# Adding the squared chunks in pairs on GpSimd ahead of the column sums of five norms

## The chip, the cores and the metric

The kernel runs on one core of a Trainium2 chip. The metric is device time in microseconds (us) of that core. The core has five engines that run side by side and meet at semaphores: TensorE (PE in the profile; its weight loads are PEld), VectorE (DVE), ScalarE (ACT), GpSimd (POOL) and SyncE (SP), which here only issues transfers.

## The reference, cut to what matters

A two-layer block works on x of 256 tokens by 1024 features, all in fp32. Each layer applies three sublayers, and each sublayer begins with the same norm, so there are six norms (numbered 0 to 5 here, 3 per layer).

```
def rms_norm(x, gain):
    y = xf * lax.rsqrt(jnp.mean(xf * xf, axis=-1, keepdims=True) + EPS)
    return y * gain
...
for l in range(2):
    h = modulate(rms_norm(x, norm_g[l, 0]), sh1, sc1); x = x + 0.5 * g1 * swiglu(h, ...)
    h = modulate(rms_norm(x, norm_g[l, 1]), sh2, sc2); x = x + g2 * token_mix(h, ...)
    h = modulate(rms_norm(x, norm_g[l, 2]), sh3, sc3); x = x + 0.5 * g3 * swiglu(h, ...)
```

The mean over the 1024 features is what the change touches: the sum of the squares of eight chunks of 128 features, for each token.

## The kernel before

**Layout.** x is kept transposed in `xT`, 128 partitions by 8 chunks by 256 tokens: a partition is one feature of a chunk. A "bank" b of a norm is the pair of chunks 2b and 2b+1, because a sublayer's output for those two chunks fills PSUM bank b. Weights come in slabs of 128x2048, numbered in the order of use; each is split into a high part (`w_hi`, by ScalarE, L1005) and a low part (`w_lo = raw - w_hi`, by VectorE, L1484), and TensorE makes three products for each tile of weights.

**The way into a norm (norms 1 to 5).** When bank b of the sublayer's output is done, VectorE adds it to `xT` (L1561, two instructions for a bank). ScalarE then squares the bank into `hf` (L1029, one instruction of 128x512) and makes `xm_hi` from it (L1031, one for each chunk), and VectorE makes `xm_lo` (L1507, one for each chunk). TensorE multiplies `hf` by a 128x128 matrix of ones (L637, function `sums`), which adds over the partitions, and accumulates the eight chunks in PSUM bank 0. While the norm's factor is not known yet, TensorE already works on the first slabs with the unnormalized `xm` (function `lead`, L650). ScalarE loads a table (L1018), splits a slab (L1005) and forms the factor `rstd` (L1012, L1014), VectorE splits a slab (L1484) and then normalizes chunk by chunk (L1541, L1546).

**Where the sums stand in TensorE's order.** Norms 1, 3 and 4 follow a feed-forward: its last output block calls `sums(norm, 0)` after its tile 5 and `sums(norm, 1)` after its tile 7, and `lead` takes banks 2 and 3 after its third chunk. Norms 2 and 5 follow the token mixing: the third of the four last slabs (K_OUT+2) is followed by `sums(norm, 0, 1)`, the fourth (K_OUT+3) by `sums(norm, 2)`, and `lead` takes bank 3.

**Order.** Every engine's order is written out by hand, and every engine executes its own queue in order, so a waiting instruction holds all behind it. GpSimd builds constants at the start, masks `bias` once (L470, L471), and in each layer clears and masks a small tile (L477, L483: `affine_select` of 64x128, twice for each of four heads). Norm 0 has its own code and is not changed.

Of the kernel before, what the change touches and what calls it, by code (L numbers as in the profile page):

```python
# [11 lines left out]
ALU = mybir.AluOpType  # L12
# [3 lines left out]
DEPTH = 2  # L16
# [89 lines left out]
def build(nc, x, c, w_ada, b_ada, norm_g, w_ff_in, w_ff_out, w_in, qk_norm_g, attn_sinks, rel_bias,  # L106
# [3 lines left out]
    with ctx:  # L110
        def sb(name, shape, dt=F32):
            return ctx.enter_context(nc.sbuf_tensor(name, [P] + shape, dt))

        def sem(name):
# [10 lines left out]
        hf = sb("hf", [C, T])  # L125
# [87 lines left out]
        eps_ready, sc_saved, sqa_ready = sem("eps_ready"), sem("scores_saved"), sem("square_ready")  # L213
        ada_loaded = [sem(f"ada_loaded{i}") for i in range(4)]
        (slab_done, bank_done, hi_ready, lo_ready, ada_weighed, ada_done, ada_saved, act_steps, dve_steps, x_ready,
         sq_ready, ss_done, rstd_ready, hf_ready, hhi_ready, h_ready, silu_ready, hid_made, hid_hi_ready, hid_ready,
         consts_ready, bias_masked, fold_ready, ada_folded, ma_ready, mhi_ready, mlo_ready, xhi_ready, xlo_ready, lead_scaled, c_loaded, small_loaded, x_loaded, c_turned, turned, x_turned, par_ready, lam_ready, lam_exp,
         cond_ready, rel_saved, rel_stored, bias_loaded, rgw_loaded, rg_done, wg_loaded, alpha_done, kraw_ready, glr_saved,
         v_saved, vrow_saved, v_turned, dup_done, ksq_ready, kss_done, krs_ready, kk_ready, z_ready, l1_ready, cum_ready,
# [4 lines left out]
         S_ready, o_done, oscaled, oT_done, masks_clear, yc_ready, gth_ready, br_used, ysp_hi,  # L224
         ysp_ready, merged_hi, merged_split, turned_out, out_copied, out_turned, stored) = (sem(n) for n in (
             "slab_done bank_done hi_ready lo_ready ada_weighed ada_done ada_saved act_steps dve_steps x_ready "
             "sq_ready ss_done rstd_ready hf_ready hhi_ready h_ready silu_ready hid_made hid_hi_ready hid_ready "
             "consts_ready bias_masked fold_ready ada_folded ma_ready mhi_ready mlo_ready xhi_ready xlo_ready lead_scaled c_loaded small_loaded x_loaded c_turned turned x_turned par_ready lam_ready lam_exp "
             "cond_ready rel_saved rel_stored bias_loaded rgw_loaded rg_done wg_loaded alpha_done kraw_ready glr_saved "
             "v_saved vrow_saved v_turned dup_done ksq_ready kss_done krs_ready kk_ready z_ready l1_ready cum_ready "  # L230
# [230 lines left out]
        @block.gpsimd  # L461
        def _(pool):
            pool.memset(ident[:, :], 0.0).then_inc(consts_ready, 1)
            pool.memset(ones[:, :], 1.0).then_inc(consts_ready, 1)
            pool.wait_ge(consts_ready, 2)
            pool.affine_select(out=ident[:, :], in_=ident[:, :], compare_op=ALU.not_equal, fill=1.0,
                               base=0, pattern=[[-1, P]], channel_multiplier=1).then_inc(consts_ready, 1)

            pool.wait_ge(bias_loaded, 128)
            pool.memset(bias[0:64, :, 128:192], NEG).then_inc(bias_masked, 1)  # L470
            pool.memset(bias[64:128, :, 0:64], NEG).then_inc(bias_masked, 1)  # L471

            for n in range(4 * DEPTH):
                if n % 4 == 0:
                    pool.wait_ge(yb_ready, n + 4)
                    for half in range(2):
                        pool.memset(g_attm[64 * half:64 * half + 64, :, 64 - 64 * half:128 - 64 * half], 0.0).then_inc(masks_clear, 1)  # L477
                pool.wait_ge(att_saved, n + 1)
                if n % 4:
                    pool.wait_ge(o_done, n)  # L480
                for half in range(2):
                    rows = slice(64 * half, 64 * half + 64)
                    pool.affine_select(out=g_attm[rows, :, rows], in_=g_att[rows], compare_op=ALU.is_ge, fill=0.0,  # L483
                                       base=0, pattern=[[0, 2], [1, CH]],
                                       channel_multiplier=-1).then_inc(att_masked, 1)

        @block.tensor
        def _(pe):  # L490
# [138 lines left out]
            for l in range(DEPTH):  # L629
                k0 = SLABS * l  # L630

                def sums(norm, *banks):

                    for b in banks:
                        pe.wait_ge(sq_ready, 4 * norm + b + 1)
                        for cc in (2 * b, 2 * b + 1):
                            last = mm(ps[:, 0, 0:T], ones[:, :], hf[:, cc, :], start=cc == 0, stop=cc == C - 1)  # L637
                    if banks[-1] == 3:
                        last.then_inc(ss_done, 1)

                def lead(p, first_bank, norm, *banks):

                    pe.wait_ge(lo_ready, p + 1)
                    pe.wait_ge(mlo_ready, norm)
                    for cc in range(C):
                        pe.wait_ge(xlo_ready, C * (norm - 1) + cc + 1)
                        for t in range(2):
                            w = [slab_kn(b, p % SPLIT)[:, cc, t * P:(t + 1) * P] for b in (w_hi, w_lo)]
                            for q, (a, b) in enumerate(((w[0], xm_hi), (w[0], xm_lo), (w[1], xm_hi))):
                                last = mm(ps[:, first_bank + t, 0:T + 2], a, b[:, cc, :], start=cc == 0 and q == 0,  # L650
                                          stop=cc == C - 1 and q == 2, skip_group_check=True)
                        if cc == 2 and banks:
                            sums(norm, *banks)
                    last.then_inc(slab_done, 1)

                def ff(f, q):
# [3 lines left out]
                    def out_block(p, j, hid, final=False):  # L660
                        pe.wait_ge(lo_ready, p + 1)
                        pe.wait_ge(hid_ready, hid)
                        for t in range(C):
                            last = slab_tile(p, t, ps[:, t // 2, (t % 2) * T:(t % 2 + 1) * T],
                                             (hid_h[j % 2], hid_l[j % 2]), n=2, rows=True, clear=j == 0 and t % 2 == 0)
                            if final and t in (1, 3, 5):
                                last.then_inc(bank_done, 1)
                            if final and t in (5, 7) and norm + 1 < 3 * DEPTH:
                                if t == 7:
                                    last.then_inc(slab_done, 1)  # L670
                                sums(norm + 1, (t - 5) // 2)
                        if not final or norm + 1 == 3 * DEPTH:
                            last.then_inc(slab_done, 1)
# [78 lines left out]
                for i in range(4):  # L752
                    n = 4 * l + i
# [95 lines left out]
                for i in range(4):  # L849
                    n = 4 * l + i  # L850
# [67 lines left out]
                for m in range(4):  # L918
                    p = k0 + K_OUT + m
                    if m == 0:  # L920
                        by_chunks(p, m, (h_hi, h_lo), merged_split, 4 * l, 2)
                    else:
                        if m >= 2:
                            pe.wait_ge(br_used, 12 * l + 12)
                        product(p, m, (h_hi, h_lo), group=pair_group(l) if m == 2 else None)
                    if m == 2:
                        sums(3 * l + 2, 0, 1)
                    if m == 3:
                        sums(3 * l + 2, 2)
# [1038 lines left out]
```

## Time and profile before

| what | value |
|---|---|
| runs | 1540.5, 1542.37, 1543.71 us, median 1542.37 us |
| the profiled execution, its time | 1542.24 us |
| its span, from the first to the last instruction | 1540.5 us |
| TensorE busy | 1507.8 us, 98% of the span |
| VectorE busy | 1140.4 us, 74% |
| ScalarE busy | 800.3 us, 52% |
| GpSimd busy | 25.2 us, 2% |
| mean granted TensorE clock | 0.992 of 2.4 GHz |

The span is shorter than the time by 1.7 us, which lie around it. Busy shares are means over stages with different limits; which engine sets the pace at a given place is read from what the others wait for there.

### The profile page before, as it was taken

Reading aid. Unit: us, or ns where it says so; the run is one execution under the profiler, and the core shown is the slowest. Engines: PE = TensorE matmul, PEld = TensorE weight load, DVE = VectorE, ACT = ScalarE, POOL = GpSimd, SP = SyncE. Lnnn points to the kernel's source line nnn. Section 1 sums busy time; section 2 is a strip of 40 time slices with the busy share of each in tenths; the row PEclk is TensorE's granted clock in tenths of the full one; section 3 lists DMA queues with packets and bytes.
Section 4 is the critical chain, followed back from the end, with each engine's and each line's share of the span. In section 5 each row is a group of like instructions: output and inputs, shape, how many; then the busy total and the mean of one; then the engine's idle time right before and its main releaser. Section 6 shows DMA issues by size and latency. Waiting matters only on the chain.

```text
span 1540.5 us, 29168 instructions
## 1 busy us (share of the span) xinstructions
PE 1507.8 (98%) x12530; PEld 1462.0 (95%) x12530; DVE 1140.4 (74%) x1547; ACT 800.3 (52%) x970; POOL 25.2 (2%) x29
## 2 busy tenths in 40 slices
PE   6999999999999999999999999999999999999998
PEld 5999998999999999999999999999999899999998
DVE  6697777898546998776877768769865589977454
ACT  4344346888546446433464444677855544464342
POOL 0000000000100000000000000000001000000000
PEclk8899999999999999999999999999999999999999
DMA  9989864554456995888658785555454589676551
GB/s 322 321 264 275 273 189 145 151 171 138 138 164 227 308 312 192 270 273 291 204 193 292 260 295 168 152 164 151 140 163 147 174 303 340 221 252 202 168 194 54
DMA packets 287073, 333.52 MB, mean 216 GB/s; under 512 B 13084, under 2 KB 241344, under 8 KB 286944
## 3 DMA queue, kind: packets, MB, share of 16 engines
q1 hardware_dynamic: 279184, 327.40, 65.0%
q10 hardware_dynamic: 7760, 4.26, 1.2%
q8 instruction: 99, 1.62, 0.4%
q14 instruction: 30, 0.25, 0.0%
HBM read 330.23 MB, written 1.38 MB: 215 GB/s over the span
## 4 chain that ended last, share of the span: by engine, by line
PE 79%; DVE 11%; ACT 7%; issue 2%; DMA 1%; ACTq 0%; SPq 0%; DVEq 0%
PE ps L501 66%; DVE w_lo L1484 4%; PE ps L874 3%; ACT w_hi L1005 2%; DVE scratch L1380 2%; DVE hf L1541 1%; DVE h_lo L1546 1%; PE ps L789 1%; PE ps L585 1%; PE ps L545 1%; DVE xT L1561 1%; ACT L1018 1%; ACT xm L1031 1%; PE ps L735 1%; PE ps L836 1%
## 5 line engine op out<-in xcount | busy, mean ns | idle before, releaser
L501 PE MATMUL ps<-h_hi,w_hi 128*128 128x256 f32 x2320 | 653.4, 282 | 1.0 <-DVE w_lo L1484 1.0
L501 PE MATMUL ps<-h_lo,w_hi 128*128 128x256 f32 x2320 | 643.7, 277 | 0.0
L501 PE MATMUL ps<-h_hi,w_lo 128*128 128x256 f32 x2320 | 641.8, 277 | 0.0
L1484 DVE TENSOR_TENSOR w_lo<-raw,w_hi 128x2048 fp32r<-128x2048 f32 x238 | 543.5, 2286 | 114.7 <-ACT w_hi L1005 114.7
L1005 ACT ACTIVATE w_hi<-raw 128x2048 fp32r<-128x2048 f32 x237 | 452.6, 1912 | 202.8 <-PE ps L501 198.1
L501 PEld LDWEIGHTS ps<-h_hi,w_hi 128*128 128x128 f32 x2320 | 434.3, 187 | 9.0 <-issue 7.1
L501 PEld LDWEIGHTS ps<-h_lo,w_hi 128*128 128x128 f32 x2320 | 437.9, 189 | 0.5 <-issue 0.5
L501 PEld LDWEIGHTS ps<-h_hi,w_lo 128*128 128x128 f32 x2320 | 434.2, 187 | 0.0
L501 PE MATMUL ps<-xm,w_hi 128*128 128x256 f32 x1408 | 251.0, 281 | 0.0
L501 PEld LDWEIGHTS ps<-xm,w_hi 128*128 128x128 f32 x1408 | 215.1, 189 | 0.0
L501 PE MATMUL ps<-xm,w_lo 128*128 128x256 f32 x704 | 197.0, 280 | 0.0
L1380 DVE SCALAR_TENSOR_TENSOR scratch<-eyr,cond,scratch 128x512 f32<-128x512 f32 x248 | 186.3, 751 | 11.5 <-DMA eyr<-in_w_ada_dram 2.5
L1623 DVE TENSOR_TENSOR t512b<-t512a,ps 128x512 f32<-128x512 f32 x41 | 28.2, 688 | 141.8 <-issue 89.2
L501 PEld LDWEIGHTS ps<-xm,w_lo 128*128 128x128 f32 x704 | 132.7, 189 | 0.0
L501 PE MATMUL ps<-hid_hi,w_hi 128*128 128x256 f32 x384 | 108.4, 282 | 1.7 <-DVE hid_lo L1627 1.5
L501 PE MATMUL ps<-hid_lo,w_hi 128*128 128x256 f32 x384 | 106.5, 277 | 0.0
L501 PE MATMUL ps<-hid_hi,w_lo 128*128 128x256 f32 x384 | 106.2, 277 | 0.0
L501 PEld LDWEIGHTS ps<-hid_hi,w_hi 128*128 128x128 f32 x384 | 71.9, 187 | 2.3 <-DVE w_lo L1484 1.9
L501 PEld LDWEIGHTS ps<-hid_lo,w_hi 128*128 128x128 f32 x384 | 72.5, 189 | 0.1
L501 PEld LDWEIGHTS ps<-hid_hi,w_lo 128*128 128x128 f32 x384 | 71.9, 187 | 0.0
L1078 ACT ACTIVATE t512a<-ps 128x512 f32<-128x512 f32 x41 | 24.5, 598 | 86.6 <-PE ps L501 83.5
L1101 ACT ACTIVATE xm<-t512b 128x512 fp32r<-128x512 f32 x20 | 12.7, 634 | 88.8 <-DVE t512b L1623 88.8
(276 smaller groups left out, 1685.8 us busy)
## 6 DMA issues: line engine op xcount, KB each, us to landing
raw<-in_w_ff_in_dram SPq DMA_DIRECT2D x176, 512.0 KB, 4.8
eyr<-in_w_ada_dram SPq DMA_DIRECT2D x144, 512.0 KB, 7.1
raw<-in_w_in_dram SPq DMA_DIRECT2D x100, 512.0 KB, 4.7
raw<-in_w_ff_out_dram SPq DMA_DIRECT2D x88, 512.0 KB, 4.8
raw<-in_w_gate_dram SPq DMA_DIRECT2D x48, 512.0 KB, 4.6
raw<-in_w_branch_dram SPq DMA_DIRECT2D x48, 512.0 KB, 4.5
raw<-in_w_out_dram SPq DMA_DIRECT2D x16, 512.0 KB, 5.8
rgw<-in_rg_w_dram ACTq DMA_DIRECT2D x16, 128.0 KB, 2.4
```

Source lines behind the costliest of these rows:

```text
L501: last = mm(outs, a, b[:, cc, :], start=clear and cc == 0 and q == 0, stop=cc == n - 1 and q == 2, skip_group_check=True)
L545: mm(ps[:, bank, t * T:(t + 1) * T], w_of[b][:, step, t * P:(t + 1) * P], h_hi[:, step, :], start=step == 0 and b == 0 and t == 0, stop=Fa ...
L585: last = mm(to, acc[:, cols], ones[:, 0:1], start=not direct, stop=True)
L735: last = nc.tensor.transpose(ps[:, 4 + hh, b * P:(b + 1) * P], pr[:, hh, b * P:(b + 1) * P], ident[:, :])
L789: last = mm(ps[:, 2 - g, t * T:(t + 1) * T], rgw[:, g, t, :], xc[:, t, :], start=True, stop=True)
L836: last = mm(ps[rows, 7, m * T:(m + 1) * T], g_qe[:, ch * CH:(ch + 1) * CH], g_S[:, ch - 1, :], start=False, stop=True, skip_group_check=True)
L874: last = mm(ps[:, 1, m * T:(m + 1) * T], a, b, start=cc == 0 and q == 0, stop=cc == C - 1 and q == 2)
L1005: f(w_hi[:, p % SPLIT, :], raw[:, p % RAW, :], ACT.Copy).then_inc(hi_ready, 1)
L1078: f(t512a[:, :], ps[:, 4, :], ACT.Silu).then_inc(silu_ready, 1)
L1380: ins = stt(acc, w[:, cc, :], by, acc, ALU.mult, ALU.add)
L1484: tt(w_lo[:, p % SPLIT, :], raw[:, p % RAW, :], w_hi[:, p % SPLIT, :].bitcast(F32), ALU.subtract).then_inc(lo_ready, 1)
L1623: tt(t512b[:, :], t512a[:, :], ps[:, 5, :], ALU.mult).then_inc(hid_made, 1)
```

## The change

For norms 1 to 5 and banks 0 to 2, GpSimd adds the second squared chunk of the bank onto the first, in place in `hf` (128x256 fp32, two inputs in SBUF). TensorE multiplies only that sum by the ones, one logical matmul for a bank in place of two; it waits for the new semaphore `sq_added` in place of `sq_ready`. Bank 3 stays as it was, with two matmuls. That makes fifteen adds, and five logical matmuls for a norm in place of eight. Each add also waits for the one before it. On GpSimd's queue the adds of norm 1 stand behind the two memsets of `bias`, those of norms 2 to 4 between the masks of layer 0 and those of layer 1, and those of norm 5 at the end.

```diff
+            def squares_added(norm):
+                for b in range(3):
+                    pool.wait_ge(sq_ready, 4 * norm + b + 1)
+                    if norm > 1 or b:
+                        pool.wait_ge(sq_added, 3 * (norm - 1) + b)
+                    pool.tensor_tensor(hf[:, 2 * b, :], hf[:, 2 * b, :], hf[:, 2 * b + 1, :], ALU.add).then_inc(sq_added, 1)
+
             for n in range(4 * DEPTH):
                 if n % 4 == 0:
+                    for norm in range(3 * (n // 4) - 1, 3 * (n // 4) + 2):
+                        if norm == 1:
+                            pool.wait_ge(bias_masked, 2)
+                        if norm == 2:
+                            pool.wait_ge(att_masked, 2 * n)
+                        if norm > 0:
+                            squares_added(norm)
+                    pool.wait_ge(sq_added, 9 * (n // 4) + 3)
                     pool.wait_ge(yb_ready, n + 4)
...
+            pool.wait_ge(att_masked, 8 * DEPTH)
+            squares_added(3 * DEPTH - 1)
...
                 def sums(norm, *banks):
                     for b in banks:
-                        pe.wait_ge(sq_ready, 4 * norm + b + 1)
-                        for cc in (2 * b, 2 * b + 1):
+                        if b < 3:
+                            pe.wait_ge(sq_added, 3 * (norm - 1) + b + 1)
+                        else:
+                            pe.wait_ge(sq_ready, 4 * norm + 4)
+                        for cc in ((2 * b,) if b < 3 else (6, 7)):
                             last = mm(ps[:, 0, 0:T], ones[:, :], hf[:, cc, :], start=cc == 0, stop=cc == C - 1)
```

## Rows read from the trace of the kernel before

**Rows 1.** The page: busy time of each engine; the chain that ended last.

```profile
PE 1507.8 (98%) x12530; PEld 1462.0 (95%) x12530; DVE 1140.4 (74%) x1547; ACT 800.3 (52%) x970; POOL 25.2 (2%) x29
...
PE 79%; DVE 11%; ACT 7%; issue 2%; DMA 1%; ACTq 0%; SPq 0%; DVEq 0%
```

**Rows 2.** TensorE's line L637: ns min/median/max; idle us before it, times.

```profile
L637 PE MATMUL ps<-hf,ones x80: 377/379/483, 230.9 to 1349.6; 128*128 128x256 f32 x80
...
  ACT hf L1029: 6.5, 8
```

**Rows 3.** Timeline of TensorE, norm 1: start, us, what, [idle before].

```profile
230.94 1.02 PE L637 MATMUL ps<-hf,ones 128*128 128x256 f32 x4
...
231.92 0.28 PE L501 MATMUL ps<-hid_lo,w_hi 128*128 128x256 f32 x1
...
251.72 0.39 PE L501 MATMUL ps<-h_hi,w_hi 128*128 128x256 f32 x1 [0.50 <-DVE w_lo L1484]
```

**Rows 4.** Timeline of TensorE in norms 4 and 5: its waits at their ends.

```profile
998.86 0.38 PE L501 MATMUL ps<-h_hi,w_hi 128*128 128x256 f32 x1 [0.49 <-DVE w_lo L1484]
...
1365.78 0.35 PE L501 MATMUL ps<-hid_hi,w_hi 128*128 128x256 f32 x1 [0.76 <-DVE hid_lo L1627]
```

**Rows 5.** The chain that ended last, norm 3: start, us, what.

```profile
787.86 0.89 DVE xm L1507 x2
...
809.41 2.59 PE ps L501 x20
```

**Rows 6.** The chain that ended last, norm 2.

```profile
599.37 0.80 DVE xT L1561 x2
...
618.71 21.31 PE ps L501 x181
```

**Rows 7.** Timeline of ScalarE, norm 1: the squares of banks 0 and 1.

```profile
229.28 0.63 ACT L1029 ACTIVATE hf<-xT 128x512 f32<-128x512 f32 x1 [1.96 <-DVE xT L1561]
...
230.67 0.63 ACT L1029 ACTIVATE hf<-xT 128x512 f32<-128x512 f32 x1
```

**Rows 8.** Timeline of VectorE, norm 1.

```profile
230.55 0.87 DVE L1507 SCALAR_TENSOR_TENSOR xm<-xT,ma,xm 128x256 fp32r<-128x256 f32 x2
231.73 0.89 DVE L1507 SCALAR_TENSOR_TENSOR xm<-xT,ma,xm 128x256 fp32r<-128x256 f32 x2 [0.31 <-ACT xm L1031]
```

**Rows 9.** Timeline of TensorE, norm 2.

```profile
591.06 1.13 PE L637 MATMUL ps<-hf,ones 128*128 128x256 f32 x4 [1.14 <-ACT hf L1029]
592.38 1.13 PE L637 MATMUL ps<-hf,ones 128*128 128x256 f32 x4 [0.19 <-ACT hf L1029]
...
593.47 0.28 PE L501 MATMUL ps<-h_lo,w_hi 128*128 128x256 f32 x1
...
598.80 0.27 PE L501 MATMUL ps<-h_hi,w_lo 128*128 128x256 f32 x1
```

**Rows 10.** Timeline of VectorE, norm 2.

```profile
590.52 2.29 DVE L1484 TENSOR_TENSOR w_lo<-raw,w_hi 128x2048 fp32r<-128x2048 f32 x1
592.73 1.67 DVE L1507 SCALAR_TENSOR_TENSOR xm<-xT,ma,xm 128x256 fp32r<-128x256 f32 x4
594.31 0.87 DVE L1561 SCALAR_TENSOR_TENSOR xT<-ps,gcol,xT 128x256 f32<-128x256 f32 x2
```

**Rows 11.** GpSimd's line L483: duration in ns min/median/max of its 16 instructions.

```profile
L483 POOL TENSOR_SCALAR_AFFINE_SELECT scratch<-scratch x16: 287/1355/2422, 387.0 to 1216.4; 64x128 f32<-64x128 f32 x16
```

**Rows 12.** Timeline of GpSimd, then of VectorE, at the first two of these 16.

```profile
386.96 2.77 POOL L483 TENSOR_SCALAR_AFFINE_SELECT scratch<-scratch 64x128 f32<-64x128 f32 x2 [3.94 <-DVE scratch L1862]
...
387.30 2.28 DVE L1484 TENSOR_TENSOR w_lo<-raw,w_hi 128x2048 fp32r<-128x2048 f32 x1
```

**Rows 13.** GpSimd's groups of instructions by line: busy us, mean ns.

```profile
L471 POOL MEMSET bias<- 64x1024 f32 x1 | 1.0, 952 | 0.1
...
L477 POOL MEMSET scratch<- 64x128 f32 x4 | 0.8, 199 | 880.0 <-DVE eyr L1717 879.9
L466 POOL TENSOR_SCALAR_AFFINE_SELECT ident<-ident 128x128 f32<-128x128 f32 x1 | 0.3, 292 | 0.2 <-POOL ones L464 0.2
```

More of the change, by code:

```diff
@@ L215, in build @@
         (slab_done, bank_done, hi_ready, lo_ready, ada_weighed, ada_done, ada_saved, act_steps, dve_steps, x_ready,
-         sq_ready, ss_done, rstd_ready, hf_ready, hhi_ready, h_ready, silu_ready, hid_made, hid_hi_ready, hid_ready,
+         sq_ready, ss_done, rstd_ready, sq_added, hf_ready, hhi_ready, h_ready, silu_ready, hid_made, hid_hi_ready, hid_ready,
          consts_ready, bias_masked, fold_ready, ada_folded, ma_ready, mhi_ready, mlo_ready, xhi_ready, xlo_ready, lead_scaled, c_loaded, small_loaded, x_loaded, c_turned, turned, x_turned, par_ready, lam_ready, lam_exp,
@@ L226, in build @@
              "slab_done bank_done hi_ready lo_ready ada_weighed ada_done ada_saved act_steps dve_steps x_ready "
-             "sq_ready ss_done rstd_ready hf_ready hhi_ready h_ready silu_ready hid_made hid_hi_ready hid_ready "
+             "sq_ready ss_done rstd_ready sq_added hf_ready hhi_ready h_ready silu_ready hid_made hid_hi_ready hid_ready "
              "consts_ready bias_masked fold_ready ada_folded ma_ready mhi_ready mlo_ready xhi_ready xlo_ready lead_scaled c_loaded small_loaded x_loaded c_turned turned x_turned par_ready lam_ready lam_exp "
```

## The prediction

> **What bounds the kernel now.** I read the page first. TensorE is busy in 98% of the span and makes 79% of the chain that ended last, VectorE and ScalarE 18% together [rows 1]. From that alone every matmul saved would be time saved, so the question is whether the removed matmuls lie in the 79% or in the rest. The second view is the sums' own line: 80 matmul records for 40 logical ones (an fp32 matmul is recorded twice), and 6.5 us of TensorE's idle time stands before them, waiting for ScalarE's squares [rows 2]. The third is the timeline of TensorE, and the chain, through each of the five norms. The reader is to see there that TensorE is not the last one anywhere in a norm. Norm 1: TensorE runs without a gap from the sums on and then sits 0.50 us until VectorE's `w_lo` at 251.72 [rows 3]. Norms 4 and 5 end in the same kind of wait, 0.49 and 0.76 us [rows 4]. In norm 3 the chain comes back to TensorE at 809.41, and in norm 2 at 618.71, each time from VectorE's `hid_lo`; in norm 2 it holds no matmul from 599.37 until there [rows 5, 6]. The path through a norm is VectorE's residual, ScalarE's square and `xm`, the table, the split of a slab, and VectorE's normalization, and line L637 is not on it. TensorE fills that time with `lead` and waits at the end.
>
> **What is removed.** Three logical matmuls for a norm, fifteen in all. Two of them (four records) begin at 230.94, the second matmul behind them at 231.92, and matmuls behind it are 0.12 us apart, so two take 231.92 - 0.12 - 230.94 = 0.86 us, one 0.43 us [rows 3]. Fifteen are 6.45 us of TensorE, 1.29 us for a norm. In each norm they end before the wait that closes it, and TensorE waits longer by as much. I count the saving as 0; the cover is the VectorE-ScalarE path of each norm, and if it were gone the 6.45 us would come back. The one place where earlier matmuls feed that path is the output of bank 3: in norms 1, 3 and 4 it is done 0.43 us sooner, but VectorE takes banks 2 and 3 back to back, so it starts nothing sooner.
>
> **What an add costs.** No row shows a two-input operation on GpSimd. From below: memset takes 952 ns for 1024 columns and 199 ns for 128, that is 0.84 ns a column, or 0.31 us for 256 without any read [rows 13]. From above: `affine_select` takes 292 ns for 128 columns with one read [rows 13]; 256 columns are 0.58 us if time goes with the columns, and 1.1 us if the second operand costs as much again. I take 0.6 us, because that is the nearest row scaled by the columns only, and keep 0.3 and 1.1 for the range. With the semaphore each add brings its data about 0.64 us after its start. The Trainium skill's "GPSIMD Engine Reference", section "Elementwise — side-by-side cycle accounting", gives 4497 ns for a two-input add of 2048 fp32 columns; my estimate from it is 0.56 us for 256, no run here shows it, and the sum below would be 0.3 us less.
>
> **When GpSimd may start.** The second `affine_select` of each head takes 2422 ns against 287 of the first [rows 11]. At the first pair, GpSimd begins at 386.96, the second instruction therefore near 387.25, and the pair ends at 389.73; VectorE's `w_lo` subtraction, two inputs in SBUF, runs from 387.30 to 389.58 [rows 12]. All eight pairs repeat this, so I read it as a wait: GpSimd's read stands still until VectorE's two-input instruction is over. The Trainium skill's "SBUF — State Buffer", section "Who interferes with whom", says that a VectorE instruction with two SBUF inputs and a GpSimd instruction that reads SBUF exclude each other for the whole instruction, whoever comes second; the trace agrees where VectorE is first, 2.42 us in place of 0.29, and does not show the other order. Without the rule's other half the second term of the sum below would be 0 and the time 1546.2 us.
>
> **Norms 2 and 5.** Bank 0 is squared by about 591.03, when TensorE starts on it, bank 1 by about 592.35 [rows 9]. VectorE has been in `w_lo` since 590.52 and stays there until 592.81; then come four `xm_lo` (L1507, `xT` and `xm_hi`, again two inputs in SBUF) until 594.40, and only then the residual, which reads PSUM and one SBUF tensor [rows 10]. So the first add can't begin before 592.81. Two cases from there. If GpSimd gets its turn at 592.81, add 0 ends at 593.42; add 1 follows at once or after one `xm_lo` of 0.40 us and ends between 594.05 and 594.46. If VectorE's next instruction, which starts at 592.73 before the last one is over, keeps GpSimd out, add 0 runs from 594.40 to 595.0 and add 1 until 595.6. TensorE's last sum for these banks then starts near 594.1 to 594.5, or 595.65. Behind it in TensorE's queue stands the whole slab K_OUT+3: with 0.11 us of restart and 0.43 us for one sum it begins at 594.6 to 595.0, or 596.2, against 593.35 now (the second matmul at 593.47 less 0.12), and its last matmul, now over at 599.07, moves with it [rows 9]. VectorE is free for the residual of bank 3 at 599.37 and could otherwise have begun it at 599.1 [rows 6], so 0.3 us of the delay is hidden. The price by this path is 1.0 to 1.4 us in the first case and 2.6 us in the second. In the first case VectorE's four `xm_lo` also move back by two adds, 1.2 us; that path arrives at the same residual, so the two don't add up, but 1.2 is the least. I take 2.0 us between the two cases, as the trace decides for neither. What is late next is ScalarE's square and `xm` of bank 3, the table, `rstd`, and TensorE at 618.71, all on the chain. Norm 5 has the same rows, so this term is 2 x 2.0 = 4.0 us. With an add of 0.3 us and the first case it is 2 x 0.6, with 1.1 us and the second 2 x 3.6.
>
> **Norms 1, 3 and 4.** In norm 1 the square of bank 0 ends at 229.91, that of bank 1 at 231.30 [rows 7]. Add 0 runs beside a residual and ends at about 230.55, just as `xm_lo` starts, and TensorE wants its sum at 230.94: nothing is late. Add 1 waits for the `xm_lo` pair until 231.42 and ends near 232.05; TensorE wants it only twelve matmuls after 231.8, near 233.2 now [rows 3] and 0.43 us sooner after. But VectorE's next `xm_lo` is due at 231.73 [rows 8], and if exclusion works both ways it starts 0.35 us late. That pair is on the chain, in norm 3 as the piece at 787.86 [rows 5]. Bounds: 0 if GpSimd never holds VectorE up or the add is short, 1.3 us if the add takes 1.1 us, as then add 0 also pushes the first pair by 0.5. I take 0.35 us, since a two-input VectorE instruction held GpSimd for its full length. Add 2 begins while VectorE is in a residual or waits for `xm_hi`, and what it may push there is followed by further such waits. Three norms make 1.05 us.
>
> **The rest at nothing.** GpSimd's queue: the adds of norm 2 wait behind masks done long before, and the masks of layer 1 behind the adds of norm 4, made two stages earlier. No DMA is issued, moved or passed on any queue. Bank 3 keeps its two matmuls and its wait.
>
> **The sum.** 1542.24 (the profiled execution, span 1540.5 and 1.7 around it) + 4.0 + 1.05 + 0 = 1547.3 us. That execution lies 0.13 us under the median of the runs, so I leave it unshifted: plus 5 us, or 0.33%.
>
> **Rivals.**
> *No change (the other side).* The mechanism is that GpSimd reads beside VectorE without waiting, the 2.4 us of [rows 11] being something else. Then add 1 ends at 593.0, the slab begins at 593.55 in place of 593.35, and these 0.2 us are hidden under the 0.3: 1542.2 us. For it: GpSimd is otherwise free. Against: eight pairs out of eight end with VectorE's instruction. It decides from the point at which add 1 ends by 593.0.
> *The saving arrives.* All fifteen matmuls shorten the path: 1542.24 - 6.45 = 1535.8 us; by parts of it 1538. For it: TensorE makes 79% of the chain. Against: the closing waits of [rows 3 to 6].
> *Costly adds.* 1.1 us for an add and the late turn in norms 2 and 5: 2 x 3.6 + 3 x 1.3 = 11 us, 1553.3 us. For it: no two-input row exists. A flip in norm 3, where add 2 is ready just ahead of a `w_lo` and would otherwise wait 2.3 us for it, adds under 1 us and is of this kind.
>
> **How the numbers follow.** Adds held by VectorE, at my sizes: 0.65, own range 1543.6 to 1550. No change 0.17. Saving 0.10. Costly adds 0.08. A range of 1541.6 to 1551.0 us leaves out the saving and most of the costly case. 0.2% (3.1 us) is about what a measurement of this kernel can tell from no change. Slower by more than that: most of the first case, which falls below it when the adds are short and GpSimd gets its turn early (0.08 of its 0.65), and the costly one, 0.65. Within: 0.25. Faster: 0.10.
>
> **What would show it.** In the changed profile L637 should have 50 records, and TensorE's timeline in norm 2 a wait before the second sum, put down to GpSimd, that is 1.1 to 2.9 us longer than 0.19; the adds should begin when a `w_lo` or `xm_lo` ends. In norms 1, 3 and 4 the second `xm_lo` pair starts about 0.35 us later. The waits that close the norms grow by up to 1.3 us in norms 1 and 4 and open in norm 3. The prediction is wrong if GpSimd's first add in norm 2 starts before 592.8 on that scale, if VectorE's `xm_lo` doesn't move, or if a norm ends with no wait of TensorE.

## The result and the profile after

The changed kernel takes 1550.34 us (median of 5 runs, 1548.34 to 1551.12) against 1543.44 us before (5 runs, 1540.5 to 1543.87). The ratio is 1.0047 with a 95% interval of 1.0036 to 1.0058, which is 7.3 us slower (the medians differ by 6.9). The forecast was 1547.3 us, slower, in a range of 1541.6 to 1551.0.

**How the loss is laid out over the norms.** The two profiled executions differ by 8.1 us of span, but they already differ by 1.5 us before the changed code runs for the first time. So I use one landmark in each norm, the start of VectorE's first residual of it (L1561 before, L1582 after), and compare the distances between landmarks. The table does that for every kernel of this study; a column holds what passes from a norm's first residual to the next norm's, less the same of the kernel before.

| kernel | norm 1 | norm 2 | norm 3 | norm 4 | norm 5 | sum |
|---|---|---|---|---|---|---|
| changed kernel | +0.13 | +2.95 | -0.06 | +0.19 | +3.35 | +6.56 |
| e1, adds in norms 1, 3, 4 | +0.07 | -0.01 | -0.08 | +0.19 | +0.01 | +0.18 |
| e2, adds in norms 2, 5 | -0.05 | +3.03 | -0.22 | +0.02 | +3.50 | +6.28 |
| e3, fewer matmuls, no adds | -0.07 | +0.40 | -0.30 | +0.14 | 0.00 | +0.17 |
| e4, adds to a tile nobody reads | +0.12 | +1.25 | -0.13 | +0.29 | +1.15 | +2.68 |
| e5, TensorE's wait filled | +0.51 | +1.36 | 0.00 | +0.48 | +1.34 | +3.69 |
| e6, sums moved, with adds | +0.51 | +1.15 | +0.01 | +0.57 | +1.12 | +3.36 |
| e7, sums moved, no adds | +0.31 | +0.33 | -0.29 | +0.11 | +0.02 | +0.48 |
| e8, reordered, no adds | +0.02 | -2.75 | -0.29 | +0.11 | -3.08 | -5.99 |
| e9, reordered, with adds | +0.16 | -2.55 | -0.06 | +0.24 | -2.54 | -4.75 |
| e10, `w_lo` in pieces, with adds | +0.23 | +3.15 | -0.06 | +0.44 | +1.68 | +5.44 |
| e11, reordered, fewer matmuls | -0.04 | -3.55 | -0.34 | +0.46 | -3.65 | -7.12 |

These are single profiled executions. A norm that an edit doesn't touch moves by up to 0.5 us from one to the next, so only the entries of 1 us and more are read one by one.

The page's busy times and chain, changed kernel, against [rows 1]:

```profile
PE 1506.6 (97%) x12500; PEld 1460.1 (94%) x12500; DVE 1144.0 (74%) x1547; ACT 800.4 (52%) x970; POOL 41.4 (3%) x44
...
PE 71%; issue 16%; DVE 5%; ACT 5%; POOL 1%; DMA 1%; ACTq 0%; SPq 0%; DVEq 0%; POOLq 0%
```

TensorE has 30 records fewer and is busy for only 1.2 us less; GpSimd is new on the chain. The 16% of "issue" is no new idle time: two stretches of 119.39 us, ahead of the first adds of norms 2 and 5, make 239 us of it, because the profile finds nothing that released those adds and the chain steps over TensorE's work there. The lines of `hf` in the trace (ns min/median/max), against [rows 2, 13]:

```profile
L658 PE MATMUL ps<-hf,ones x50: 377/379/793, 232.5 to 1357.5; 128*128 128x256 f32 x50
...
L479 POOL TENSOR_TENSOR hf<-hf x15: 726/736/2819, 231.6 to 1348.7; 128x256 f32<-128x256 f32 x15
```

An add takes 0.74 us when nothing is in its way, and up to 2.82 us. GpSimd's timeline shows where; the first row lies in norm 1, the second is adds 0 and 1 of norm 2, the third add 2 of norm 3:

```profile
232.90 0.74 POOL L479 TENSOR_TENSOR hf<-hf 128x256 f32<-128x256 f32 x1 [0.57 <-ACT hf L1050]
...
592.80 3.13 POOL L479 TENSOR_TENSOR hf<-hf 128x256 f32<-128x256 f32 x2 [119.40 <-issue]
...
795.05 2.82 POOL L479 TENSOR_TENSOR hf<-hf 128x256 f32<-128x256 f32 x1 [2.21 <-ACT hf L1050]
```

VectorE's timeline in norm 2, which answers to [rows 10], all of it 1.65 us later by the landmark:

```profile
592.18 2.29 DVE L1505 TENSOR_TENSOR w_lo<-raw,w_hi 128x2048 fp32r<-128x2048 f32 x1
594.39 2.61 DVE L1528 SCALAR_TENSOR_TENSOR xm<-xT,ma,xm 128x256 fp32r<-128x256 f32 x4
...
603.86 0.88 DVE L1582 SCALAR_TENSOR_TENSOR xT<-ps,gcol,xT 128x256 f32<-128x256 f32 x2 [1.72 <-PE ps L519]
```

The record of add 0 starts at 592.80, in the middle of `w_lo`, and ends at 595.07 (the chain gives it 2.27 us alone), which is 0.60 us after `w_lo` does. An undisturbed add takes 0.74 us, so the record holds a wait: the add was ready at 592.80 and got its turn when `w_lo` ended. That was ahead of the four `xm_lo`, which now take 2.61 us in place of 1.67. Add 1 follows until 595.93. The last residual, which VectorE came to by itself before, now waits 1.72 us for TensorE. TensorE in norm 2, against [rows 9]:

```profile
595.11 0.70 PE L658 MATMUL ps<-hf,ones 128*128 128x256 f32 x2 [3.53 <-POOL hf L479]
595.98 1.08 PE L658 MATMUL ps<-hf,ones 128*128 128x256 f32 x2 [0.17 <-POOL hf L479]
596.50 0.78 PE L519 MATMUL ps<-h_hi,w_hi 128*128 128x256 f32 x1
597.07 0.42 PE L519 MATMUL ps<-h_lo,w_hi 128*128 128x256 f32 x1
597.29 0.41 PE L519 MATMUL ps<-h_hi,w_lo 128*128 128x256 f32 x1
...
599.73 0.28 PE L519 MATMUL ps<-h_hi,w_lo 128*128 128x256 f32 x1
...
603.55 0.27 PE L519 MATMUL ps<-h_hi,w_lo 128*128 128x256 f32 x1
```

The reader is to see two things. The wait ahead of the sums is 3.53 us in place of 1.14. And the matmuls behind it stand 0.21 us apart and last 0.41 us, until they go back to 0.12 and 0.28 near 599.6. The same in stretches (busy us of PE, PEld, DVE, ACT and POOL, then the granted clock, 1.00 being 2.4 GHz and 0.50 1.2 GHz, then DMA):

```profile
591.00:595.00 4.00, 0.57 (x5) 0.37 (x4) 4.00 (x6) 4.00 (x8) 2.20 (x1) 1.00 0.50 177
595.00:597.00 2.00, 1.72 (x5) 1.15 (x6) 2.00 (x5) 1.58 (x1) 0.78 (x2) 0.79 0.65 171
597.00:599.00 2.00, 2.00 (x12) 2.00 (x11) 0.91 (x3) 1.18 (x3) 0.47 (x1) 0.50 1.12 382
599.00:601.00 2.00, 2.00 (x16) 2.00 (x16) 2.00 (x3) 0.25 (x1) 0.26 (x1) 0.86 1.01 373
```

**The account of norm 2.** On the scale shifted by 1.65 us the second sum used to start at 594.03 and now starts at 595.98: +1.95. From there to the end of the slab it was 599.07 - 592.38 = 6.69 us with two sums, so 6.26 with one, and is 603.82 - 595.98 = 7.84: the clock costs 1.58. Together 1.95 - 0.43 + 1.58 = 3.10 us, of which 0.27 us are hidden as forecast. The landmark says 2.95.

### The profile page after: what moved, and what is told of

The parts are those of the page before. It is cut to its first block, busy times and chain, and to the rows that moved or that the text cites. A ratio compares the mean times of both kernels' runs of the same rounds, so it can differ in the third digit from the quotient of the medians.

```text
span 1548.6 us, 29140 instructions
## 1 busy us (share of the span) xinstructions
PE 1506.6 (97%) x12500; PEld 1460.1 (94%) x12500; DVE 1144.0 (74%) x1547; ACT 800.4 (52%) x970; POOL 41.4 (3%) x44
## 4 chain that ended last, share of the span: by engine, by line
PE 71%; issue 16%; DVE 5%; ACT 5%; POOL 1%; DMA 1%; ACTq 0%; SPq 0%; DVEq 0%; POOLq 0%
PE ps L519 59%; PE ps L895 3%; DVE w_lo L1505 2%; ACT w_hi L1026 1%; PE ps L810 1%; DVE hf L1562 1%; DVE h_lo L1567 1%; PE ps L756 1%; ACT L1039 1%; PE ps L671 1%; ACT xm L1052 1%; POOL hf L479 1%; PE ps L563 1%; PE ps L799 1%; ACT pr L1160 0%
```

## The experiments

**e1 and e2: where is the loss?** The change is split by norm.

```diff
+ADDED = (1, 3, 4)        # e1; (2, 5) in e2
...
-                        if b < 3:
-                            pe.wait_ge(sq_added, 3 * (norm - 1) + b + 1)
+                        if norm in ADDED and b < 3:
+                            pe.wait_ge(sq_added, 3 * ADDED.index(norm) + b + 1)
...
-                        for cc in ((2 * b,) if b < 3 else (6, 7)):
+                        for cc in ((2 * b,) if norm in ADDED and b < 3 else (2 * b, 2 * b + 1)):
```

> The adds on GpSimd in norms 1, 3 and 4 only; norms 2 and 5 as in the kernel before. Theory (the loss sits in norms 2 and 5, where the first add waits for VectorE's w_lo and TensorE then waits for the add): within 0.5 us of the kernel before, as the three norms moved by 0.13, -0.06 and 0.19 us between the two profiles. Rival (every add costs something, spread over all five norms): +3 to +4.5 us, three fifths of the whole loss.

Measured: ratio 1.0007 (0.9998 to 1.0016), which is 1.1 us and not told from nothing; +0.18 us by the landmarks. The rival asked for 3 us or more.

> The adds on GpSimd in norms 2 and 5 only. Theory: +6 to +6.6 us on the kernel before, 2.95 us in norm 2 and 3.35 us in norm 5, with a TensorE wait of about 3.5 us in each and a granted clock of 0.5 for some 3 us behind it. Rival (spread over all norms): +2.5 to +3 us.

Measured: ratio 1.0044 (1.0031 to 1.0056), 6.8 us, and +6.28 us by the landmarks, with a wait of 3.76 us ahead of the sums of norm 2 and a clock of 0.50 behind it. The loss is in norms 2 and 5.

**e3: what are the fifteen matmuls worth?** The kernel before, without them and without adds.

```diff
-                        for cc in (2 * b, 2 * b + 1):
+                        for cc in ((2 * b,) if b < 3 else (6, 7)):
```

> The fifteen matmuls are gone and nothing is put in their place: banks 0 to 2 contribute one squared chunk in place of two, so the norm's factor leaves out three of the eight chunks. Theory (TensorE is not the last one in any norm, so its 6.45 us are worth nothing): the time of the kernel before, within 0.7 us; the waits that close the norms grow by up to 1.3 us each. Rival (the saving is real and the adds cost 13 us): -6.45 us, 1536 to 1537.

Measured: ratio 1.0003 (0.9994 to 1.0011). TensorE's timeline at the ends of norms 1, 2 and 3 shows where the 1.29 us of each went. Norm 1 stands against [rows 3]; of the kernel before, the ends of norms 2 and 3 are:

```profile
618.71 0.35 PE L501 MATMUL ps<-hid_hi,w_hi 128*128 128x256 f32 x1 [0.75 <-DVE hid_lo L1627]
...
809.41 0.36 PE L501 MATMUL ps<-hid_hi,w_hi 128*128 128x256 f32 x1
```

And of e3, the ends of norms 1, 2 and 3:

```profile
252.65 0.39 PE L501 MATMUL ps<-h_hi,w_hi 128*128 128x256 f32 x1 [0.79 <-DVE w_lo L1484]
...
619.59 0.36 PE L501 MATMUL ps<-hid_hi,w_hi 128*128 128x256 f32 x1 [1.62 <-DVE hid_lo L1627]
...
810.69 0.36 PE L501 MATMUL ps<-hid_hi,w_hi 128*128 128x256 f32 x1 [1.43 <-DVE hid_lo L1627]
```

The waits were 0.50, 0.75 and under 0.2 us. In norms 2 and 3 they grow by 0.9 and some 1.3 us. In norm 1 the closing wait grows by 0.3 only; the rest goes further up. Counted from the landmark, TensorE is 1.28 us ahead of the kernel before when `lead` ends. It then waits 0.18 us for `h_lo` at 244.41, where it begins on the normalized chunks (0.34 us at 245.17 in the changed kernel), and is 0.95 us ahead. From there a chunk takes it 0.79 us in place of 0.69, which is VectorE's pace (0.40 us each for `hf` and `h_lo` in the chain): 0.44 us are left after the chunks, 0.29 us at the closing wait, and none behind it.

**e4: adds that nobody waits for.** GpSimd makes all fifteen adds, into a part of `scratch`; TensorE's side is that of the kernel before. VectorE's `norm` also waits for them, as it overwrites their inputs; they are long over by then.

```diff
-                    pool.tensor_tensor(hf[:, 2 * b, :], hf[:, 2 * b, :], hf[:, 2 * b + 1, :], ALU.add)...
+                    pool.tensor_tensor(scratch[:, 0:T], hf[:, 2 * b, :], hf[:, 2 * b + 1, :], ALU.add)...
```

> GpSimd makes the same fifteen adds at the same places but writes them to a tile that nobody reads; TensorE waits for the squares and makes all eight matmuls of a norm, as before. Theory (what hurts is that TensorE waits for the adds, not that they hold VectorE up): at most +1.5 us, as in norms 2 and 5 VectorE's four xm_lo move back by about 1 us and its w_lo ahead of the last residual has no slack, up to +0.9 us a norm, and 0.1 to 0.2 us in norms 1, 3 and 4. If all of the loss came from VectorE being held up: +6 to +7 us. If none: 0.

Measured: ratio 1.0017 (1.0008 to 1.0026), 2.6 us, more than the +1.5 that I had as the most. By the landmarks 1.25 us in norm 2 and 1.15 us in norm 5. VectorE's timeline in norm 2:

```profile
590.73 2.29 DVE L1502 TENSOR_TENSOR w_lo<-raw,w_hi 128x2048 fp32r<-128x2048 f32 x1
592.94 2.63 DVE L1525 SCALAR_TENSOR_TENSOR xm<-xT,ma,xm 128x256 fp32r<-128x256 f32 x4
...
597.45 1.07 DVE L1525 SCALAR_TENSOR_TENSOR xm<-xT,ma,xm 128x256 fp32r<-128x256 f32 x2 [1.10 <-ACT xm L1049]
```

The two adds cost the first four `xm_lo` 0.96 us, and add 2 costs the next pair 0.18 us (1.07 for 0.89): 1.14 us of a chain that is VectorE's own. So GpSimd does hold VectorE up.

**e5: the same wait, with TensorE busy.** Fourteen bf16 matmuls on constants into an unused bank stand ahead of `sums(norm, 0, 1)` in norms 2 and 5.

```diff
                     if m == 2:
+                        for _ in range(14):
+                            mm(ps[:, 5, :], ones[:, :].bitcast(BF16)[:, 0:P],
+                               ones[:, :].bitcast(BF16).unsqueeze(1).broadcast_to((P, 2, T)), start=True, stop=True)
                         sums(3 * l + 2, 0, 1)
```

> The changed kernel with fourteen bf16 matmuls of 128x512 on constants, into a PSUM bank that is free, ahead of sums(norm, 0, 1) in norms 2 and 5: they fill about 3.0 us of TensorE's 3.5 us wait and delay nothing. Theory (half of the loss in these norms is the granted clock, which falls to 0.5 behind the wait): the clock stays at 1.0, the slab behind the sums takes 5.8 us in place of 7.3, and the time is 2.5 to 3.5 us less than that of the changed kernel, so +3.5 to +4.5 us on the kernel before. Rival (the clock is a bystander, the add's lateness alone is the loss): +6.5 to +7.

Measured: ratio 1.0025 (1.0015 to 1.0035), 3.9 us. Against the 1.0047 of the changed kernel that is 3.4 us given back, and the intervals don't overlap. TensorE's timeline and the stretches of norm 2:

```profile
591.25 3.20 PE L949 MATMUL ps<-ones 128*128 128x512 bf16 x14
594.94 0.70 PE L658 MATMUL ps<-hf,ones 128*128 128x256 f32 x2 [0.50 <-POOL hf L479]
```

```profile
595.00:597.00 2.00, 1.83 (x10) 1.37 (x11) 2.00 (x5) 1.41 (x1) 0.73 (x1) 1.00 0.70 208
597.00:599.00 2.00, 2.00 (x19) 2.00 (x19) 0.90 (x3) 1.35 (x3) 0.64 (x1) 1.00 1.09 358
```

The sum starts as late after the landmark as in the changed kernel (594.94 - 590.42 = 4.52 against 595.11 - 590.58 = 4.53), and the clock stays at 1.00. By the landmarks norm 2 goes from +2.95 to +1.36 and norm 5 from +3.35 to +1.34: 1.6 and 2.0 us are the clock's, and what is left is close to what e4 shows for VectorE alone.

**e6 and e7: does the place of the sums matter?** The sums of banks 0 and 1 move behind the last slab, with the adds (e6) and without (e7).

```diff
-                    if m == 2:
-                        sums(3 * l + 2, 0, 1)
                     if m == 3:
-                        sums(3 * l + 2, 2)
+                        sums(3 * l + 2, 0, 1, 2)
```

> The changed kernel with the sums of banks 0 and 1 of norms 2 and 5 moved behind slab K_OUT+3, next to that of bank 2; the adds stay. Theory (the adds hurt where TensorE's slab K_OUT+3 is queued behind their wait): the wait and the clock drop are gone, what stays is VectorE held up, as in the run with the adds aside: +1 to +3 us on the kernel before. Rival (GpSimd's adds hurt wherever their sums stand): +5 to +7.

Measured: ratio 1.0017 (1.0008 to 1.0027), 2.6 us. TensorE has a wait of 1.25 us for add 2 in norm 2 and one of 1.47 us for ScalarE's last square, and the clock stays at 1.00 behind both. Norms 2 and 5 lose 1.15 and 1.12 us, as with the adds aside.

> The kernel before with the same move of the sums, no adds. Theory: TensorE finishes slab K_OUT+3 some 3.4 us sooner, but VectorE comes to the last residual no sooner, as its w_lo stands ahead: the time of the kernel before, within 0.7 us. Rival (TensorE's order limits): -2 to -7 us.

Measured: ratio 1.0000 (0.9991 to 1.0009). TensorE's slab is done sooner and nothing comes of it.

**e8: shorten VectorE's path instead.** If VectorE's order is the limit, then the last residual, for which TensorE is ready early in e7, should go ahead of work that nobody waits for yet. The edit stands on top of e7's move of the sums.

```diff
                     if m == 2:
                         lo(k0 + K_OUT + 4)
                         expand_low(3 * l + 2, 0, 1)
-                    if m == 3:
-                        lo(k0 + K_OUT + 5)
                     residual(m, slab_done, k0 + K_OUT + m + 1)
-                    if m > 1:
-                        expand_low(3 * l + 2, m)
+                expand_low(3 * l + 2, 2)
+                lo(k0 + K_OUT + 5)
+                expand_low(3 * l + 2, 3)
```

> The kernel before with the sums moved behind slab K_OUT+3 and VectorE's residual of bank 3 ahead of the xm_lo of bank 2 and of the w_lo of slab K_OUT+5, in norms 2 and 5. Theory (the path through the norm is VectorE's order, not TensorE's amount of work): the residual of bank 3 comes about 3.4 us sooner, and after the other limits each norm gives back 2 to 3.4 us: -4 to -6.8 us, 1535 to 1538. Rival (another chain takes over at once): within 1.5 us of the kernel before.

Measured: 1536.36 us, ratio 0.9964 (0.9951 to 0.9976), 5.6 us faster than the kernel before and the fastest version here that computes everything. VectorE's order was not changed without e7's move, so what it gives alone is not shown; TensorE's slab K_OUT+3, which the last residual needs, ended 0.3 us ahead of that residual in the kernel before. The chain of norm 2 is now TensorE's throughout, against [rows 6]:

```profile
586.82 8.57 PE ps L501 x72
595.38 2.59 PE ps L637 x12
597.97 2.17 PE ps L650 x18
600.14 0.86 PE ps L637 x4
601.01 9.39 PE ps L650 x78
```

**e9 and e11: adds, and fewer matmuls, on the reordered kernel.** The same edits of the sums as in the changed kernel (e9) and in e3 (e11), on top of e8.

> The reordered kernel (sums of norms 2 and 5 behind slab K_OUT+3, VectorE's last residual ahead of the xm_lo of bank 2 and the w_lo) with GpSimd's fifteen adds. Theory (an add that becomes ready while VectorE is in xm_lo or w_lo waits for its end, and here add 2 of norms 2 and 5 becomes ready just then): add 2 ends 2 to 3 us after TensorE wants it, so +4 to +7 us on the reordered kernel without adds, 1540 to 1544. Rival (with VectorE's path shortened TensorE is the last one and the saved matmuls count): -1 to -3 us on it, 1533 to 1535.

Measured: 1537.64 us, ratio 0.9975 (0.9965 to 0.9984): 1.1e-3 of 1542, or 1.7 us, above e8's 0.9964 (1.2 us by the landmarks), with intervals that overlap. Neither theory held: TensorE waits 1.59 us for add 2 in norm 2 and not the 2 to 3 us ahead of its need that I had worked out. Add 2 becomes ready at 597.86, when VectorE is 0.04 us from the end of its last residual, and ends at 598.58, ahead of the `w_lo` that starts at 599.19. I had worked it out as ready only once `xm_lo` had begun; with both residuals back to back, that pair starts later.

> The reordered kernel without adds and without the fifteen matmuls; as in the earlier run of that kind, three of eight squared chunks are left out of the norm's factor. Theory (after the reordering TensorE and VectorE finish norms 2 and 5 within 0.3 us of each other, and norms 1, 3 and 4 are VectorE's as before): 0 to -1 us on the reordered kernel. Rival (the matmuls now lie on the path): -2.6 us for norms 2 and 5, up to -6.45 us for all.

Measured: 1535.01 us, ratio 0.9957 (0.9944 to 0.9969), 1.1 us under e8 by the ratios, whose intervals overlap, and 1.1 us by the landmarks, at the edge of what was expected. Norms 2 and 5 read 0.80 and 0.57 us lower than in e8, little more than what an untouched norm moves by. So even where TensorE is the chain, six matmuls of 0.43 us return about 1.4 us of 2.6, and VectorE's path ends right behind: in e11 TensorE waits 0.42 us for `hid_lo` at the end of norm 2.

**e10: shorten what GpSimd waits for.** In the changed kernel the `w_lo` that runs when the first square is ready is cut into four instructions of 512 columns.

```diff
                     if m == 2:
-                        lo(k0 + K_OUT + 4)
+                        in_pieces(k0 + K_OUT + 4, 4)
```

> The changed kernel with VectorE's w_lo of slab K_OUT+4, the one that runs when the first square of norms 2 and 5 is ready, cut into four instructions of 512 columns. Theory (GpSimd's read waits for the one VectorE instruction that is running): the first add ends by about 1.5 us sooner on the same scale, TensorE's wait ahead of the sums falls from 3.5 to about 2 us, the clock stays up or falls for less, and the time is 2 to 4.5 us under the changed kernel, +2.5 to +5 us on the kernel before. Rival (GpSimd's lateness has another cause than the length of VectorE's instruction): no gain, +6.5 to +7.5 us.

Measured: ratio 1.0035 (1.0022 to 1.0049), 1.9 us under the changed kernel, with intervals that overlap. GpSimd, VectorE and TensorE in norm 2, one row of each:

```profile
591.51 2.39 POOL L479 TENSOR_TENSOR hf<-hf 128x256 f32<-128x256 f32 x2 [119.41 <-issue]
```

```profile
590.89 3.56 DVE L1512 TENSOR_TENSOR w_lo<-raw,w_hi 128x512 fp32r<-128x512 f32 x4
```

```profile
592.82 2.36 PE L658 MATMUL ps<-hf,ones 128*128 128x256 f32 x4 [2.54 <-POOL hf L479]
```

Both adds now fall inside the four pieces, which take 3.56 us in place of 2.29. GpSimd is through in 2.39 us instead of 3.13, and TensorE's wait falls by 1.0 us. That the length of VectorE's running instruction sets the add's start is borne out. The first piece ended only 0.07 us after add 0 was ready, and the add did not get its turn there; it ends at 592.77, 0.59 us after the second piece. That is 1.0 us sooner behind the landmark than in the changed kernel, and not the 1.5 expected. The time is another matter, and here the expectation that the clock would stay up or fall for less failed. The stretches of norm 2:

```profile
590.00:593.00 3.00, 0.47 (x4) 0.26 (x3) 3.00 (x6) 3.00 (x7) 1.35 (x2) 0.91 0.69 208
593.00:599.00 6.00, 6.00 (x23) 5.19 (x24) 4.90 (x11) 3.72 (x6) 1.63 (x2) 0.50 0.57 184
```

The clock is at 0.50 for all of TensorE's work up to 599.3, some 6.5 us, against 3.4 us behind the longer wait of the changed kernel, and norm 2 loses as much as ever (+3.15). In norm 5, behind a wait of 2.98 us, it is low for 3.4 us in place of 5.3, and that norm gains (+1.68).

## Why the prediction was right

- **The matmuls are worth nothing.** Counted at 0; e3 measures 1.0003. The argument from the closing waits held (in norm 1 the time went into waits for `h_lo` as well), and e8 shows its other side: the path through norms 2 and 5 was VectorE's order.
- **An add costs 0.6 us.** It is 0.74; the bounds 0.3 and 1.1 held it.
- **GpSimd's first add waits for `w_lo`.** Shown in the changed kernel (ready at 592.80, over 0.60 us after `w_lo`) and by e10. On the scale shifted by 1.65 us add 0 ends at 593.42, as forecast, and TensorE's last sum for these banks starts at 594.33, inside 594.1 to 594.5. The sign named for being wrong, a start before 592.8 on that scale, is met by the record's 591.15, but that record holds the wait, so its end decides. TensorE's longer wait stands ahead of the first sum (3.53 us for 1.14), not ahead of the second (0.17 for 0.19) as written. Of the two cases the first came true: GpSimd gets its turn between two VectorE instructions, even when the next is due at once.
- **Norms 2 and 5, 2 x 2.0 us.** Measured 2.95 and 3.35. This is the term that was off. The first case, which came true, was priced at 1.0 to 1.4 us, and e4, e5 and e6 measure 1.1 to 1.4 us for it. That VectorE's path and TensorE's wait arrive together and don't add up was right too: VectorE held up alone (e4, 1.25 and 1.15 us) costs nearly the same as with TensorE's wait on top at full clock (e5, 1.36 and 1.34). The step that failed is the one that let the slab behind the wait run at its old pace. It ran partly at 1.2 GHz, 1.6 to 2.0 us a norm, and the sum had no term for that. With the first case at 1.2 us the sum would have had 2.4 us for the two norms; taking the middle of two cases made it 4.0 and hid 1.6 of the 3.9 us that were missing.
- **Norms 1, 3 and 4, 3 x 0.35 us.** Measured 0.13, -0.06 and 0.19, not told from nothing (e1). The place was right and VectorE is held up, but the second pair starts where it did, 3.36 us behind the landmark, and takes 0.18 us longer: VectorE's next instruction starts at 233.25 and add 1 is over only at 233.64 (232.90 + 0.74), so it does not wait for the add's end. The row is below.
- **The flip in norm 3** happened: add 2 was ready at 795.05 and `w_lo` had started at 795.01, so it took 2.82 us and TensorE waited 1.65 us. It cost nothing, since TensorE had about that much to spare in norm 3 (1.43 us in e3), 1.29 us of it from the removed matmuls. I had priced it as a loss of up to 1 us. It also used up the cover: the chain below stays on TensorE from this wait to the norm's end, which has no wait. A norm that ends so was named as a sign of being wrong, and in norm 3 it is one: there the removed matmuls did count, and paid for the add.
- **The sum.** Forecast +5.05, measured +6.56 by landmarks and +7.3 by the ratio. That it came this near is in part luck: 3.6 us of clock stood at nothing, while norms 2 and 5 had 1.6 us too much by the choice between two cases and norms 1, 3 and 4 had 0.8 us too much. 1550.34 us lies above the range that I gave the case itself, up to 1550, and inside the stated one only because that took in a part of the costly case, which did not come.

The chain in norm 3 of the changed kernel, from add 2 on; it holds TensorE alone from 797.92:

```profile
795.05 2.83 POOL hf L479
...
797.92 1.56 PE ps L658 x6
799.49 9.38 PE ps L671 x78
...
814.50 7.51 PE ps L519 x65
```

VectorE's timeline in norm 1 of the changed kernel, against [rows 8]; the add runs from 232.90 to 233.64:

```profile
233.25 1.07 DVE L1528 SCALAR_TENSOR_TENSOR xm<-xT,ma,xm 128x256 fp32r<-128x256 f32 x2 [0.25 <-ACT xm L1052]
```

## What to carry to other kernels

A busy share of 98% does not say that work taken off that engine is time saved; look at which wait closes the stage that the work stands in. Work moved to GpSimd must be placed against VectorE's long two-input instructions, and what is queued behind the consumer's wait is what it costs. If a change opens a wait of some microseconds on TensorE, price the clock behind it as well as the wait. A shorter wait need not mean a smaller price of the clock (e10). In this kernel the gain was in the order, not in TensorE's load: with the sums moved behind the last slab, which alone gave nothing (e7), one residual moved ahead of two `xm_lo` and a `w_lo` gave 5.6 us.

## What the runs showed of the hardware beyond the forecast

**TensorE's clock falls behind one wait of a few microseconds.** In the changed kernel TensorE stood 3.53 us in norm 2, took up work at a granted clock of 1.00, fell to 0.50 near 596.2, about 1 us into it, and came back near 599.6, some 3.4 us later. In norm 5, after 3.74 us, and in e10, after 2.54 us, its clock was already at 0.50 when it took up work or fell at that moment. How long it stayed low while TensorE worked did not follow the wait: 6.5 us behind 2.54 us (e10, norm 2), 3.4 behind 2.98 (e10, norm 5), 3.4 behind 3.53 and 5.3 behind 3.74 (changed kernel). Waits of 1.14 us (kernel before), 1.59 us (e9) and 1.65 us (norm 3 of the changed kernel) left it at 1.00. The price in the changed kernel was 1.6 us and 2.0 us. With TensorE kept busy in the wait (e5) it stayed at 1.00. The Trainium skill's "TensorE: Matmul & The Clock Gate", section "What's actually happening", says that the gate follows how busy TensorE has been recently; the trace agrees, with 1.00 under e5's filler and 0.50 without it.

**GpSimd and VectorE hold each other up both ways, but an add does not hold VectorE for its whole record.** The Trainium skill's "SBUF — State Buffer", section "Who interferes with whom", has the loser blocked for the whole of the other's instruction. An add behind a `w_lo` does wait until the end. In the other order VectorE lost less than the add's remaining time: 0.18 us of 0.39 for a pair in norm 1, and 0.94 us in norm 2, where 0.60 us of add 0 and the 0.73 us of add 1 stood in its way. Why it gets in before the add's recorded end was not tried; that the add has read its inputs by then and is only writing would fit.
